# A hybrid decoder layer on one core: the u and Q projections as three passes on split operands, and the key search regrouped

## The reference, cut to what matters

```python
u, q, k, v, qi, ki, wi, gates = split(rms_norm(x) * ln1 @ w_in)      # u: 512 columns, q: 512
a_pool = pool_mixer(u)             # trailing means over 2, 4, 8, 16 tokens minus u, a linear map
s = sum_h wi[h] * relu(qi[h] @ ki.T)                                 # index scores, 4 heads
idx = top_k(causal(s), 256)                                          # for each query
a_attn = softmax(q @ k[idx].T / 8 + bias) @ v[idx]                   # 8 heads of 64
m = sigmoid(gates_1) * (a_pool @ w_pool_proj) + sigmoid(gates_2) * (a_attn @ w_attn_proj)
h = x + m @ w_out
y = rms_norm(h + (silu(f_1) * f_2) @ w_down)                         # f = rms_norm(h) * ln2 @ w_gate_up
```

## Time and profile before

| | us |
|---|---|
| time, median of 3 runs | 1624.27 (1621.79 to 1626.20) |
| the profiled execution, its own time | 1626.26 |
| its span, first to last instruction | 1624.6 |
| TensorE busy in the span | 1554.4 (96%) |
| VectorE busy | 946.4 (58%) |
| POOL busy | 597.1 (37%) |
| ACT busy | 559.4 (34%) |
| mean granted clock of TensorE | 0.984 |

### The profile page before, as it was taken

The page is one execution under the profiler, slowest core; times in us unless marked ns, Lnnn a source line. Parts: engine busy times, 40 slices in busy tenths (PEclk is TensorE's granted clock), DMA queues, the critical chain, the costliest instruction groups (busy, mean ns, idle before and its releaser), DMA issues.

```text
span 1624.6 us, 25488 instructions
## 1 busy us (share of the span) xinstructions
PE 1554.4 (96%) x9345; PEld 1360.6 (84%) x9345; DVE 946.4 (58%) x2161; ACT 559.4 (34%) x1156; POOL 597.1 (37%) x546
## 2 busy tenths in 40 slices
PE   7998999979999988999999999999999999999997
PEld 4553466647997566999899899999999999999997
DVE  3215898897997665422536855554454555555546
ACT  2113364414423655322334514224223133242233
POOL 2101007365544321211121737336355264373450
PEclk9999999998898999999999999999999999999999
DMA  5531011033110001421011302102011021020103
GB/s 173 99 108 53 7 40 41 20 91 85 40 40 14 2 2 42 120 81 47 27 40 40 104 27 78 44 34 77 26 52 52 26 77 52 26 77 26 52 1 117
DMA packets 91041, 87.56 MB, mean 54 GB/s; under 512 B 17214, under 2 KB 81358, under 8 KB 90957
## 3 DMA queue, kind: packets, MB, share of 16 engines
q1 hardware_dynamic: 79591, 73.74, 14.8%
q0 software_dynamic: 3392, 9.97, 2.7%
q10 hardware_dynamic: 7982, 2.83, 0.7%
HBM read 78.30 MB, written 8.45 MB: 53 GB/s over the span
## 4 chain that ended last, share of the span: by engine, by line
PE 57%; DVE 1%; POOL 1%; issue 1%; ACT 0%; POOLq 0%; DVEq 0%
PE banks L1938 27%; PE banks L2035 15%; PE banks L108 13%; DVE yo L2512 0%; PE banks L1895 0%; PE banks L1876 0%; PE banks L2052 0%; POOL wL L2086 0%; ACT XH L2154 0%; POOL hnL_lo L2099 0%; DVE hnL_hi L2367 0%; POOL dL L2083 0%; POOL T4L L2099 0%; ACT sH L2147 0%; ACT resid L2151 0%
## 5 line engine op out<-in xcount | busy, mean ns | idle before, releaser
L2086 POOL TENSOR_TENSOR wL<-w_raw,wH 128x512 fp32r<-128x512 f32 x176 | 230.8, 1322 | 314.9 <-ACT wH L2197 313.8
L1938 PE MATMUL banks<-hnH,wH 128*128 128x344 f32 x704 | 225.8, 321 | 2.2 <-POOL wL L2086 0.8
L1938 PE MATMUL banks<-hnH,wL 128*128 128x344 f32 x704 | 224.7, 319 | 0.0
L2499 DVE TENSOR_TENSOR resid<-resid,banks 128x344 f32<-128x344 f32 x264 | 132.1, 512 | 96.7 <-PE banks L2035 96.7
L2035 PE MATMUL banks<-aH,dH 128*128 128x344 f32 x528 | 169.3, 321 | 0.0
L2035 PE MATMUL banks<-aH,dL 128*128 128x344 f32 x528 | 169.1, 320 | 0.0
L2035 PE MATMUL banks<-aL,dH 128*128 128x344 f32 x528 | 168.2, 319 | 0.0
L1391 DVE TENSOR_SCALAR_CACHE_REDUCE pta<-SC,thr 128x384 uint8<-128x384 f32 (+4 forms) x160 | 144.0, 930 | 2.2 <-POOL SC L867 0.2
L2197 ACT ACTIVATE wH<-w_raw 128x512 fp32r<-128x512 f32 x176 | 109.7, 627 | 73.1 <-PE banks L1938 40.4
L1938 PEld LDWEIGHTS banks<-hnH,wH 128*128 128x128 f32 x704 | 132.1, 188 | 3.2 <-issue 1.9
L1938 PEld LDWEIGHTS banks<-hnH,wL 128*128 128x128 f32 x704 | 132.3, 188 | 0.0
(11 more groups left out here) (393 smaller groups left out, 3522.7 us busy)
## 6 DMA issues: line engine op xcount, KB each, us to landing
w_raw<-in_w_gate_up_dram SPq DMA_DIRECT2D x22, 1024.0 KB, 5.0
d_raw<-in_w_down_dram SPq DMA_DIRECT2D x11, 1024.0 KB, 4.9
big<-in_w_in_dram SPq DMA_DIRECT2D x12, 512.0 KB, 3.9
W<-in_x_prompt_dram SPq DMA_DIRECT2D x8, 512.0 KB, 6.9
slab_raw<-in_w_in_dram SPq DMA_DIRECT2D x8, 512.0 KB, 4.1
x_nat<-in_x_prompt_dram SPq DMA_DIRECT2D x8, 512.0 KB, 3.7
slab_raw<-in_w_out_dram SPq DMA_DIRECT2D x8, 512.0 KB, 3.9
out_dram<-yo SPq DMA_DIRECT2D x8, 512.0 KB, 2.6
```

The lines of the kernel that those rows point to most:

```text
L1938: last = mm(out, W_[w][s][:, i * P:(i + 1) * P], x_of(x)(i), start=start and i == 0 and j == 0, stop=stop and i == HALF - 1 and j == 2)
L2086: gp.tensor_tensor(wL[s].rearrange("p (k n) -> p k n", k=HALF), quadrant(x, *HOME[name]), f32(wH[s]).rearrange("p (k n) -> p k n", k=HALF) ...
L2499: V.tensor_tensor(resid[:, m, chunk(DOWN_ORDER[o])], resid[:, m, chunk(DOWN_ORDER[o])], ps[:, 4 + n % 4, 0:CH], ALU.add).then_inc(y_done, 1)
```

## The change

What it does, in five parts.

- **Split input.** During the index scores ACT rounds each of the 24 pieces of `hT` (`high_xq`), POOL subtracts (`low_xq`, into `XLq`, which lies where the weights of keys and index were), and ACT writes the high part over `hT` as `XH` (`keep_xq`). Small tables that lay in `Z` move to `late`.
- **Split weights and three passes.** Each slab is split in two halves of four tiles: ACT rounds (`high_half`), POOL subtracts (`low_half`), into two rings of 4 halves each. TensorE runs `half_product(n, h)`: for all 3 chunks 4 tiles x 3 passes in the type float32r. A chunk is complete only after the second half. The slab's DMA waits for the low parts, not for the products.
- **Restoring.** After the last u/Q product POOL adds `XH` and `XLq` back into `hT`, 8 pieces of 1032 (`restore_x`): five before the key gathers, one amid them, two after. The gate's split then works on `hT` as before.
- **Search.** Block 4 leaves the rounds of sample and block 5 and joins blocks 6 and 7: 4 rounds (`ROUNDS_FIRST`) before the one-hot step of the list, 4 after the masks of blocks 2, 3 and 5, 24 after the sample softmax. The mask of block 4 follows these; the masks of blocks 6 and 7 move into the attention loop, one step in each of units 16 to 25.
- **Order on TensorE.** `sum_sample_ties` stands before the first half of slab 7, `sum_lanes` between its halves, `turn_ranks` after them, all ahead of the linear map of the mixer; `list_keys` comes at chunk 4, `begin_sample_logits` at chunk 7.

The diff, cut to its core (counter offsets for the later waits and the placing of tables left out):

```diff
 # SP
-                        sp.wait_ge(uq_ready, 3 * (n - 1))
+                        sp.wait_ge(slab_lo, 2 * (n - 1))
                     load_slab(n % 2, slice(C_U + n * P, C_U + (n + 1) * P))
 # TensorE
-                    for k in range(KD):
-                        last = mm(ps[:, x % 6, 0:CH], big[:, n % 2, k, :], hT[:, k, chunk(c)], start=k == 0, stop=k == KD - 1)
+                def half_product(n, h):
+                    pe.wait_ge(slab_lo, 2 * n + h + 1)
+                    hi, lo = half_slab(n, h)
+                    for c in range(NCH):
+                        x = NCH * n + c
+                        if h == 0 and x >= 6:
+                            pe.wait_ge(uq_evac, x - 5)
...
+                        for k in range(4):
+                            for a, (w, v) in enumerate(((hi, XH), (hi, XLq), (lo, XH))):
+                                last = mm(ps[:, x % 6, 0:CH], w[:, k * P:(k + 1) * P], v[:, 4 * h + k, chunk(c)],
+                                          start=h == 0 and k == 0 and a == 0, stop=h == 1 and k == 3 and a == 2)
+                        if h == 1:
+                            last.then_inc(uq_ready, 1)
+                for n in range(U_ITEMS + Q_ITEMS):
+                    if n == 0:
+                        pe.wait_ge(xh_done, 12)
+                    if n == 1:
+                        transpose_sample_scores()
+                    if n == 7:
+                        sum_sample_ties()
+                    half_product(n, 0)
+                    if n == 0:
+                        join_sample_heads()
+                        pe.wait_ge(xh_done, 24)
...
+                    if n == U_ITEMS:
+                        transpose_state()
+                        transpose_last_u()
+                    if n == 7:
+                        sum_lanes()
+                    half_product(n, 1)
+                turn_ranks()
...
-                    if g == 0:
-                        sum_sample_ties()
...
-                before = {0: [sum_lanes], 1: [turn_ranks], 5: [list_keys], 8: [begin_sample_logits],
+                before = {4: [list_keys], 7: [begin_sample_logits],
 # POOL
                 for i in range(FIRST_TOPK, NBLK):
+                    for u in range(IH * (i - FIRST_TOPK), IH * (i - FIRST_TOPK + 1)):
+                        low_xq(u)
                     if i - FIRST_TOPK + 4 < NB:
                         load_kid(i - FIRST_TOPK + 4)
+                    if i == NBLK - 1:
+                        for n in range(2):
+                            for h in range(2):
+                                low_half(n, h)
                     hide_later_keys(i)
+                for n in range(2, 6):
+                    for h in range(2):
+                        low_half(n, h)
                 pool.wait_ge(uq_evac, 3 * U_ITEMS)
...
                     pool.wait_ge(pooled, g + 1)
+                    if g in (1, 2):
+                        for h in range(2):
+                            low_half(5 + g, h)
+                pool.wait_ge(uq_ready, 3 * (U_ITEMS + Q_ITEMS))
+                for k in range(5):
+                    restore_x(k)
                 pool.wait_ge(sm_step, STEP["list"])
                 for c in range(16):
+                    if c == 8:
+                        restore_x(5)
                     gp.indirect_dma_start(picked[:, c, :], ...
+                restore_x(6)
+                restore_x(7)
 # ACT
                 for n in range(PROMPT_UNITS):
                     relu_scores(n)
+                    high_xq(n)
+                    if n:
+                        keep_xq(n - 1)
+                    if n >= PROMPT_UNITS - 4:
+                        high_half((n - PROMPT_UNITS + 4) // 2, n % 2)
...
+                keep_xq(PROMPT_UNITS - 1)
                 copy_sample_keys(NB - 1)
...
                 for x in range(2, 3 * U_ITEMS):
                     sign_rounds(x)
                     u_out(x)
+                    if x % NCH == NCH - 1:
+                        for h in range(2):
+                            high_half(x // NCH + 2, h)
 # VectorE
-                    count(0, 4, cntB[:, 32:33])
...
                 early_rounds(1)
+                for r in range(ROUNDS_FIRST):
+                    search_round(SECOND, (4, 6, 7), r)
                 dve.wait_ge(sm_made, SM["ranks_turned"])
...
-                for k, i in enumerate((2, 3, 4, 5)):
+                for k, i in enumerate((2, 3, 5)):
                     to_mask(k, i)
...
-                for r in range(ROUNDS_AHEAD, BITS):
-                    pair_round(slice(5, 7), (6, 7), r)
-                settle(slice(5, 7))
+                for r in range(ROUNDS_FIRST + ROUNDS_AHEAD, BITS):
+                    search_round(SECOND, (4, 6, 7), r)
+                settle(SECOND)
+                to_mask(3, 4)
...
-                for k, i in ((4, 6), (5, 7)):
-                    for step in range(5):
-                        late_mask(k, i, step)
...
+                    if LATE_FROM <= n < LATE_FROM + 10:
+                        late_mask(4 + (n - LATE_FROM) // 5, 6 + (n - LATE_FROM) // 5, (n - LATE_FROM) % 5)
```

More of the change, by code:

```diff
@@ L388, in decoder_layer, with half_slab @@
             units = [(c, k) for ks in ((4, 5), (6, 7), (0, 1, 2, 3)) for c in range(NCH) for k in ks]
+            uq_units = [(c, k) for k in range(KD) for c in range(NCH)]
+            def half_slab(n, h):
+                ring = u_ring if n < U_ITEMS else q_ring
+                return ring[(2 * n + h) % 4], ring[4 + (2 * n + h) % 4]
             G_ORDER = (4, 5, 6, 7, 0, 1, 2, 3)
@@ L1138, in _ @@
                     A(qT[:, j, c * CH:(c + 1) * CH], ps[:, x % 6, 0:CH], ACT.Copy, scale=HD ** -0.5).then_inc(uq_evac, 1)
+                    if c == NCH - 1 and j < 2:
+                        for h in range(2):
+                            high_half(U_ITEMS + j + 2, h)
                 act.wait_ge(uq_evac, 24)
```

173 lines of the change are left out of this document (100 added, 73 removed).

## The result

| | before | after |
|---|---|---|
| time, median of 4 | 1625.24 (1621.79 to 1626.79) | 1655.90 (1651.88 to 1656.27) |
| profiled execution, span | 1624.6 | 1654.0 |
| TensorE busy | 1554.4 | 1551.2 |
| VectorE busy | 946.4 | 962.7 |
| POOL busy | 597.1 | 662.2 |

The change makes the kernel slower by 30.7 us: the ratio after to before is 1.0187 (95% interval 1.0167 to 1.0207). I had forecast 1635 in a range of 1614 to 1648; the sign was right, the size was not. TensorE's busy time falls by 3.2 us and not by the 21.4 of the sum; its mean granted clock is 0.970 instead of 0.984.

What follows compares the result with a forecast made beforehand. Two chains, TensorE's gate and VectorE's last masks, were taken to end within a microsecond before the attention. Gate +7.6 and masks +3 on 1626.26 gave 1636.9, on the median's scale 1635 us; range 1614 to 1648.

Steps and rivals of the forecast that it cites:

- the 21.4 of the sum: u and Q on TensorE: 192 products at three passes of 0.1575 us instead of 0.584 save 21.4 us, if nothing waits.
- late masks: Attention loop: VectorE gets 16.0 us of two masks in ten units, costing +3 us (0 to 16).
- I take 403: Start of the values: 403 us, against 395.44 before, from chains giving 403 (gathers) and 399 or 412 (ACT); gate at 418.
- so the gathers behind them wait in full: POOL's queue: three restores of 2.39 us, 7.2 in all, delay the gathers; first value gather at 375 us.
- Rival (c): ACT is held through the gathers again: values at 412, gate +16.6, masks +3, time 1644 us; chance 0.18.
- The index stage: Splits beside the index scores: +7 us (0 to 25.4) for the start of u and Q and of the sample rounds.
- By the sums both just fit: Index stage: ACT's added 25.4 us against 25.6 of waits, POOL's 27.4 where it was busy 8.1 of 55.
- The sample rounds: VectorE's search before the mixer: 18 rounds at 1.8 us plus 3 last 36 us, to 248; ties at 299.
- my 3.4: Fourteen sample rounds during mixing take 3.4 us each, between 2.9 and the old 3.90, as POOL's instructions hold VectorE up.
- My other sum by that rule: Index stage: if every such VectorE instruction meets a 0.94 us POOL one, it loses 10 us rather than 4; time 1641.
- The list: Ties to first key gather: four rounds over blocks 4, 6, 7 at 4.5 us, 18; first gather 343 (326 to 350).
- VectorE's end: Last masks before the attention: 24 rounds and block 4's mask end at 510.4, 3 us before TensorE's 513.4.

Runs made afterwards that it cites:

- e7b: The changed kernel with only POOL's first two low parts of the gate's input moved ahead of the value gathers: 1649.2 us, ratio 1.0166 to the kernel before.
- e7: The changed kernel with no second-search round ahead of the one-hot, four after the masks, and the first two low parts ahead of the value gathers: 1645.0 us, ratio 1.0141.
- e2: The changed kernel with all eight restores ahead of the key gathers: 1651.7 us, ratio 1.0164 to the kernel before.
- e4: The changed kernel with the four rounds after the masks, all restores ahead of the gathers and slab 7 ahead of the sums: 1648.2 us, ratio 1.0142.
- e6: The kernel before with only the search regrouped and late masks, u and Q in one fp32 product, no splits: 1641.8 us, ratio 1.0116.
- e13: e11 with restores waiting for VectorE's fourth one-hot step, block 4's mask in the attention and one search round in ACT's exp: 1642.2 us, ratio 1.0126.
- e11: The changed kernel with e7's and e10's edits, TensorE's sums and map reordered around slab 7, and restores waiting for the ranks: 1644.8 us, ratio 1.0122.
- the two single runs: The kernel before with only POOL's split subtractions, or only ACT's split copies, on data nobody reads: 1625.4 us and 1634.0 us.
- e1: The changed kernel with the four search rounds ahead of the one-hot done after the masks instead: 1650.9 us, ratio 1.0155 to the kernel before.
- e10: The changed kernel with two more of ACT's block 5 counts ahead of each copy of u from the fifth on: 1658.2 us, ratio 1.0203.

## Why the prediction fell short

Bounds and signs held: the passes go at the rate of the gate's, the saved time lay idle before slab 7, ended by VectorE, and the gate set the attention's start. A half of slab 7 took 5.76 us (313.04 to 318.80) where I had 5.7. The steps, each on the profiled execution:

| step | forecast | measured | missed by the step itself |
|---|---|---|---|
| first half product | 193.6 | 197.9 | +4 |
| sample rounds start | 212 | 216.1 | +4 |
| ties | 299 | 303.7 | +0.7 |
| mixer's map | 314 | 319.7 | +1 |
| first key gather | 343 | 351.6 | +4 |
| first value gather | 375 | 383.3 | 0 |
| gate | 418 | 437.7 | +11.4 |
| attention | 513.4 | 533.2 | 0 |
| late masks | +3 | +3.4 | +0.4 |

- **The step that failed** is "I take 403" for the values. From the first key gather (343) it leaves 60 us to the values and 75 to the gate; before took 66.7 and 81.6, after 70.9 and 86.1. Two things are wrong in it.
  - It weighed two chains, POOL's value gathers (403) and ACT's own stand (399 or 412), and overlooked a third that the code shows: `keep_x(0)` on ACT waits for `low_x(0)`, which on POOL stands behind the restores and four value gathers, and the key copy stands behind `keep_x(0)`. I wrote of the restores "so the gathers behind them wait in full", and did not follow the low parts, which are queued there too. In before that low part was never late, since ACT itself was held until 353.27. This is 4.5 of the 11 us: without the long wait the stretch to the gate takes 81.6 us (`e7b`).
  - The other 6.6 us are what 403 takes off before's own stretch, by letting ACT's stand fall away. `e7` had its first key gather where I had mine, at 343.3, and its gate came at 424.9, not at 418. In `e2`, `e4`, `e7` and `e7b` the stretch took 81.6 to 81.9 us, as before's 81.6: with all restores ahead of the gathers ACT stood for something remote (16.5 us in `e2` and `e4`), and with only two low parts moved up it waited for low parts (12.4 us in six waits in `e7`). Only `e6`, without restores, was shorter at the same clock (77.9). The 74.4 and 74.5 of `e13` and `e11` come with the values at the full clock, 8.1 us instead of 15.2. Rival (c), values 9 us later because ACT is held through the gathers, named a wait that after's trace doesn't have and that `e2`'s has. What would set the pace if neither wait were there, no run shows.
- **The index stage** was sized at 7 and split into 3 for ACT and 4 for POOL's holds. It cost 11, and the two single runs turn the split round: ACT 8.6, POOL 0.4 at TensorE (3.0 at VectorE). "By the sums both just fit" was the fault: ACT's waits for TensorE are spread over the units, and a copy of 0.49 us behind each relu delays the next relu wherever the wait was shorter. The holds themselves are there: L1497, with two inputs in SBUF, takes 1.38 us on 768 columns where before's took 1.02, while the counts, which write out their accumulator, keep their length (0.740 on 512 columns, 0.742 before). The Trainium skill, SBUF — State Buffer, section Who interferes with whom, draws the line just there: a POOL instruction that reads SBUF and one of VectorE with two SBUF inputs shut each other out for a whole instruction, so do a POOL instruction and one of VectorE in a 2-port mode, and the form with an accumulator has no such mode. In both the trace agrees. (For copies and plain tensor_scalar the page sets conditions on the operands, which the prediction left out.) My other sum by that rule (10 us for POOL's holds in this stage, 1641 in all) is nearer to the measured time by luck: what the rule lengthens was not what TensorE waited for, and POOL's part alone moved TensorE by 0.4 us.
- **The sample rounds** before the mixer: 18 took 38.0 us where I had 36, for POOL's halves of slabs held three of them (3.23 to 3.25 instead of 1.86), and the 19th took 6.39, with the wait of 3.39 for ACT. In the mixing they took 3.33, near my 3.4. The two errors all but cancel, and my 3.4 was right in part by luck: the "3.90 each" of before that it leans on was read wrong. Only 18 rounds were over at 250.93; the 19th took 6.10 us, 3.22 of them a wait for ACT's count and no hold by POOL, and the 13 behind it took 3.64 each.
- **The list**: four rounds 19.8 for 18, and the list product 6.4 instead of 3.7 at a lower granted clock (0.57) behind TensorE's wait of 6.99. `e1` confirms that TensorE's map is next behind the rounds: without them the first key gather comes only 8.5 us earlier (7.4 from the first half product), not 20.
- **VectorE's end** was forecast at 510.4 and came at 519.9. That it would have 13 us to spare was not: the gate was later still.

What stays open: `e2` is 4 us better than after by the medians while its trace has the gate at the same place. The traced execution took 1655.3, like after's 1656.0; two of the four took 1649.4 and 1649.7, and what was quicker in them no trace shows. Open too is whether POOL's work could be placed so that it holds nobody, which none of these orders did.

## What to carry to other kernels

When work is added to an engine's list, follow every instruction behind it to whoever waits for it, the small ones first: here a low part of 0.93 us behind four gathers held a copy, the copy TensorE, and TensorE the gate, for 4.5 us. And follow the waits that stay: ACT's two waits took each other's place, and the stretch around them kept its length. Idle time summed over a stage is no room for work that stands between links of a loop; measure such an addition alone, on data that nobody reads. And time saved on the busiest engine (21.4 us here by the sum) is worth nothing in such a stage until the engines that come in beside it, VectorE and POOL, get their share shorter too; both had theirs lengthened.

## What the runs showed of the hardware

VectorE's small steps that meet one of POOL's long ones end with it: in `e10` the update at 309.76 took 2.34 us and ended at 312.10, where POOL's mixer step ended at 312.08; in after the same update, at 312.94, met none and took 0.16. Made ready 3.2 us earlier, it ended 1.0 earlier. Long ones are held like short ones, and POOL is held too: 128x2048 with two inputs took 2.29 alone and 4.34 next to a restore, and five restores beside such steps took 17.79 us instead of 11.74 (`e13`). And the values ran at either level of TensorE's clock (1.2 and 2.4 GHz) after the same products, with waits of 0.3 to 1.2 us between them in the 17 us before: in `e11` at the full one,

```profile
410.97 3.76 PE L739 MATMUL banks<-I,W 128*128 128x64 f32 x32 [0.55 <-ACT W L1284]
```

where after took 14.6 us for the same two groups at the lower (granted clock 0.50 from 425 to 440); yet from the gate's start to the attention all took 95.5 us (437.74 to 533.21 in after, 419.09 to 514.56 in `e11`): what the clock gave in the values (7 us) stayed up to the gate; in the gate the first 4 us of after run at the lower level (0.50 from 437.7 to 441) and none of `e11` (1.00 from 419 to 425), and `e11` has longer waits for ACT's high parts instead (1.2 us instead of 0.4). In `e11` none of it reached the attention, since VectorE ended last.
